# Epsilon of the first block's layer norms on VectorE, and token tile 0's normed rows ahead of token tile 1's first residual

## What is computed

```python
def layer_norm(x, g, b):
    mu = jnp.mean(xf, -1, keepdims=True)
    var = jnp.mean(jnp.square(xf - mu), -1, keepdims=True)
    return ((xf - mu) * lax.rsqrt(var + LN_EPS)).astype(x.dtype) * g + b
...
for l in range(DEPTH):                       # first block
    u = x * (1.0 + sc1) + sh1
    y = mixer(u, ...)                        # holds a layer norm of its own, of the convolution's rows
    x = layer_norm(DN_ALPHA * x + (1.0 + gt1) * y, ln_mix_g[l], ln_mix_b[l])
    u = x * (1.0 + sc2) + sh2
    h = jnp.square(jax.nn.relu(u @ w_up[l])) @ w_down[l]
    x = layer_norm(DN_ALPHA * x + (1.0 + gt2) * h, ln_ffn_g[l], ln_ffn_b[l])
```

## Time and profile before

| what | value |
|---|---|
| median of 3 runs | 1811.62 us (1811.55 to 1812.15) |
| span of the profiled execution | 1813.6 us |
| TensorE busy | 1755.5 us, 97% |
| VectorE busy | 1275.5 us, 70% |
| ScalarE busy | 891.5 us, 49% |
| GpSimd busy | 57.3 us, 3% |
| mean DMA rate over the span | 191 GB/s |
| mean granted TensorE clock | 0.997 of full |

### The profile page before, as it was taken

How to read it: one execution, slowest core, us unless ns; L and a number is a source line. 1 busy time by engine, 2 the same in 40 slices (tenths; PEclk the granted TensorE clock), 3 DMA queues, 4 the chain that set the end, 5 groups by cost and what they waited for, 6 DMA issues and landing times.

```text
span 1813.6 us, 26735 instructions
## 1 busy us (share of the span) xinstructions
PE 1755.5 (97%) x9254; PEld 1450.9 (80%) x9254; DVE 1275.5 (70%) x1973; ACT 891.5 (49%) x1530; POOL 57.3 (3%) x111
## 2 busy tenths in 40 slices
PE   8999999998999999998999999999999999999998
PEld 3776778996766779987998977788889989778886
DVE  5788887667788885568557987655555588865555
ACT  1456434443455444444556664544455667544443
POOL 0000010000000000002000000000000000000000
PEclk9999999999999999999999999999999999999999
DMA  8866568774866566663665444555646645345553
GB/s 300 267 213 218 162 216 301 253 230 133 264 220 209 185 210 209 209 190 110 210 215 156 131 142 141 174 185 184 190 153 200 215 131 160 117 155 182 184 186 126
DMA packets 216040, 346.29 MB, mean 191 GB/s; under 512 B 19611, under 2 KB 113353, under 8 KB 215673
## 3 DMA queue, kind: packets, MB, share of 16 engines
q1 hardware_dynamic: 213448, 338.89, 58.3%
q0 software_dynamic: 1632, 5.39, 1.0%
q10 hardware_dynamic: 850, 0.54, 0.1%
HBM read 343.69 MB, written 1.07 MB: 190 GB/s over the span
## 4 chain that ended last, share of the span: by engine, by line
issue 79%; PE 12%; DVE 4%; DVEq 1%; POOLq 1%; POOL 1%; ACT 0%; DMA 0%; SPq 0%; ACTq 0%
PE acc L150 2%; PE acc L148 2%; PE acc L149 2%; PE prod L223 1%; PE prod L225 1%; PE prod L224 1%; DVE w_lo L134 1%; DVEq L937 1%; PE prod L148 1%; DVE proj L938 1%; PE prod L150 1%; PE prod L149 1%; PE turn L262 0%; DVE x_res L938 0%; DVE x_res L936 0%
## 5 line engine op out<-in xcount | busy, mean ns | idle before, releaser
L134 DVE TENSOR_TENSOR w_lo<-w_raw,w_hi 128x1024 fp32r<-128x1024 f32 (+2 forms) x584 | 643.7, 1122 | 308.6 <-ACT w_hi L128 302.9
L128 ACT CAST w_hi<-w_raw 128x1024 fp32r<-128x1024 f32 (+2 forms) x584 | 557.9, 968 | 406.6 <-PE acc L150 186.3
L148 PE MATMUL prod<-w_hi,hT_hi 128*128 128x512 f32 (+2 forms) x880 | 319.8, 363 | 4.7 <-ACT proj_b L1949 3.6
L150 PE MATMUL prod<-w_hi,hT_lo 128*128 128x512 f32 (+2 forms) x880 | 313.0, 356 | 0.0
L149 PE MATMUL prod<-w_lo,hT_hi 128*128 128x512 f32 (+2 forms) x880 | 312.3, 355 | 0.0
L148 PEld LDWEIGHTS prod<-w_hi,hT_hi 128*128 128x128 f32 x880 | 166.3, 189 | 25.0 <-DVE gates L2202 5.9
L150 PEld LDWEIGHTS prod<-w_hi,hT_lo 128*128 128x128 f32 x880 | 166.3, 189 | 15.4
L149 PEld LDWEIGHTS prod<-w_lo,hT_hi 128*128 128x128 f32 x880 | 166.8, 189 | 14.6
L223 PE MATMUL prod<-uT_hi,w_hi 128*128 128x256 f32 x448 | 127.1, 284 | 1.6 <-DVE w_lo L134 1.1
L148 PE MATMUL prod<-w_hi,uT_hi 128*128 128x512 f32 x304 | 124.6, 410 | 2.7 <-DVE uT_lo L301 1.3
L224 PE MATMUL prod<-uT_lo,w_hi 128*128 128x256 f32 x448 | 126.4, 282 | 0.0
(11 more groups left out here) (349 smaller groups left out, 2836.6 us busy)
## 6 DMA issues: line engine op xcount, KB each, us to landing
w_raw<-in_w_in_dram SPq DMA_DIRECT2D x72, 512.0 KB, 3.8
ada_raw<-in_w_ada_dram SPq DMA_DIRECT2D x68, 512.0 KB, 6.7
w_raw<-in_w_in_dram SPq DMA_DIRECT2D x192, 172.0 KB, 2.4
w_raw<-in_w_up_dram SPq DMA_DIRECT2D x64, 512.0 KB, 4.4
w_raw<-in_w_down_dram SPq DMA_DIRECT2D x64, 512.0 KB, 4.5
w_raw<-in_w_gate_dram SPq DMA_DIRECT2D x128, 192.0 KB, 2.6
w_raw<-in_w_ffn_gate_dram SPq DMA_DIRECT2D x88, 256.0 KB, 3.6
w_raw<-in_w_ffn_up_dram SPq DMA_DIRECT2D x88, 256.0 KB, 4.3
```

What stands on the lines that cost most here:

```text
L128: act.copy(self.hi[:, s, 0:cols], self.raw[:, s, 0:cols]).then_inc(self.hi_done, 1)
L134: dve.tensor_tensor(self.lo[:, s, 0:cols], self.raw[:, s, 0:cols], self.hi[:, s, 0:cols].bitcast(F32), ALU.subtract).then_inc(self.lo_done, 1)
L148: pe.matmul(out, a_hi, w_hi, start=first and c == 0, stop=False)
L150: mm = pe.matmul(out, a_lo, w_hi, start=False, stop=last and c == chunks - 1)
```

## The change

Three things. `norm_rstd` on GpSimd loses the addition of epsilon and the drain; the root is its only instruction and is what waits for the signal. `mean_var` on VectorE gets the addition behind a drain, and the signal now comes from the addition. And at the four boundaries both normed halves of tile 0 stand ahead of the first residual half of tile 1. (Lines behind L694 move up by two on GpSimd, ScalarE and much of VectorE, and are equal again from L933 on.)

```diff
             def norm_rstd(n, ready, done, tok):

                 pool.wait_ge(ready, n)
-                pool.tensor_tensor(var_eps[:, tok:tok + 1], mv[:, tok, 1:2], eps, ALU.add)
-                pool.drain()
                 pool.tensor_tensor(rstd[:, tok:tok + 1], var_eps[:, tok:tok + 1], half_neg, ALU.pow).then_inc(done, 1)
...
             def mean_var(tok, parts, done):

                 dve.drain()
-                dve.bn_aggr(mv[:, tok, :], stats[:, tok, 0:parts, :].rearrange("p a s -> p (a s)")).then_inc(done, 1)
+                dve.bn_aggr(mv[:, tok, :], stats[:, tok, 0:parts, :].rearrange("p a s -> p (a s)"))
+                dve.drain()
+                dve.tensor_tensor(var_eps[:, tok:tok + 1], mv[:, tok, 1:2], eps, ALU.add).then_inc(done, 1)
...
                 mix_residual(0, 0)
                 mix_residual(0, 1)
                 split(layer(l, at + 8, G1), 1)
-                mix_residual(1, 0)
                 next_u2(0, 0)
                 next_u2(0, 1)
+                mix_residual(1, 0)
                 take_u2_lo(0)
                 mix_residual(1, 1)
                 split(layer(l, at + 9, G1), 2)
```

More of the change, by code:

```diff
@@ L1037, in vector @@
                     split(layer(l, 0, G1), 1)
-                    last_residual(1, 0)
                     next_u(0, 0)
                     next_u(0, 1)
+                    last_residual(1, 0)
                     take_u_lo(0)
```

## The result

| | kernel before | kernel after |
|---|---|---|
| median of 8 runs | 1811.69 us (1809.87 to 1815.61) | 1819.84 us (1815.68 to 1822.32) |
| ratio, 95% interval | 1 | 1.0037 (1.0028 to 1.0046) |
| span of the profiled execution | 1813.6 us | 1820.5 us |
| mean granted TensorE clock there | 0.997 | 0.995 |

The change makes the kernel slower by 0.37%, which is 6.7 us (5.1 to 8.3), against a forecast of 4.2. The sign and the mechanism were right. The two medians themselves are 8.2 us apart, at the upper end of that interval. The median of the kernel after lies 1.0 us above the upper end of the range; 1.0037 times the 1811.62 of the prediction is 1818.3, just inside it. That is not the place of the forecast's own case (1815.0 to 1816.6) but of its first rival, in which TensorE's clock falls (1817 to 1819).

A forecast was written before the change was run, and what follows sets the result against it. VectorE's queue was taken to bound the four boundaries, where norms stand between big products. Epsilon 2.2, root wait 2.1, sooner transposes 0 and convolution norms -0.1 sum to +4.2 us on 1811.62: 1815.8 us, range 1813.4 to 1818.8.

The forecast's parts named there:

- the forecast's own case: Whole kernel: VectorE's longer queue at the four boundaries gives 1815.0 to 1816.6 us; chance 0.52.
- first rival: TensorE's clock falls at its longer wait for the second `w_lo`, 1 us each fall, 1817 to 1819; chance 0.19.
- The reading of the bound: At the boundaries, time added to VectorE's queue between tile 0's aggregate and the second `w_lo` adds to the program.
- The wait for the root: At each boundary VectorE waits for GpSimd's root ahead of tile 0's normed rows: 0.53 us each, 2.1 in four.
- The holding by `w_lo`: A GpSimd operation begun inside a `w_lo` is held until that ends; a root then needs 0.40 us more.
- The rival of a root that isn't held: At the boundaries the root runs under `w_lo`, so 2.1 us go away: +2.1, 1813.7 us; chance 0.13.
- The epsilon term: Additions on VectorE at four boundaries, two tiles each: two at 0.20 and six at 0.30 us, 2.2 in all.
- Sooner transposes: Tile 0's transposes can start earlier at the boundaries, but TensorE then waits longer for the second `w_lo`: gain 0.
- The convolution norms: GpSimd's chain gets shorter there, but VectorE gains two additions of 0.30 and 0.26 us: minus 0.1 us together.
- a clock under 1 near 244 or 838 us: Sign of being wrong: granted TensorE clock under 1 near 244, 445, 644 or 838 us.
- dense neighbours of a lone pause: Argument against a clock fall: TensorE's wait at the second `w_lo` has dense products as neighbours.

The follow-up runs named there:

- the late wait: Kernel after, but VectorE waits for GpSimd's root only ahead of L938, not ahead of L936: median 1816.33 us, ratio 1.0023.
- epsilon alone: Kernel before with only the epsilon addition moved from GpSimd to VectorE, order of instructions unchanged: median 1816.06 us, ratio 1.0021.
- the reordering alone: Kernel before with only tile 0's normed halves put ahead of tile 1's first residual half, epsilon still on GpSimd: median 1818.95 us, ratio 1.0039.

## Why the prediction was right, and where it was short

**The reading of the bound held.** Where the clock held, what was put into VectorE's queue between the aggregate of tile 0 and the normed rows of tile 1 came out at the end of the boundary: 0.40 for two additions of 0.13 and 0.23, 1.03 for a wait of 0.96 and the 0.08 of lost overlap, 0.54 less when the wait went. Drawing the second `w_lo` forward only moved TensorE's wait, and the 0.26 us that it added to the queue stood at the third transposes. One correction: the prediction named the second `w_lo` as the place where the queue ends; it reaches further, to tile 1's normed rows, which changed no number.

**The wait for the root** was forecast at 0.53 a boundary and 2.1 in all. The row shows 0.46 of idle time and the 0.08 of overlap, 0.54. The holding by `w_lo`, on which it rests, was shown by taking `w_lo` away: 1.47 fell to 0.56. The rival of a root that isn't held has fallen. For tile 1 the prediction allowed for a root that is held by both `w_lo`, and even that would have cost nothing; the root is held by the first alone. It begins at 243.28 inside the first and, after 1.46 us, ends at 244.74, while the second still runs (243.12 + 2.35 = 245.47).

**The epsilon term was over-sized.** Forecast 0.30 for each of six additions and 0.20 for two, 2.2 us; the rows show 0.23 and 0.13, 1.6 us. The wrong step is the time from the start of the addition to the start of what follows: I took 0.14 from a row whose successor was a copy, and `w_lo` follows after 0.07 to 0.08.

**Sooner transposes** were priced at 0, and gave 0: the late wait at equal epsilon is as long as epsilon alone, 14.86, at the one boundary where both had a full clock.

**The convolution norms** gave 0.2 and 0.1 us, 0.3 together instead of 0.1, within the bounds given.

**A term was missing.** The two pauses, 0.42 and 0.36 us, lie on the path. With 1.6 for epsilon and 2.2 for the waits they make 4.6 of the 4.75 us by which the four boundaries grew at full clock. The forecast of 4.2 was thus near that sum in part by luck, because an over-sized term stood in for an unseen one. The page before does list pauses of this kind under "issue", but nothing in it told where they would fall in the changed kernel.

**The clock was under-weighted.** As the first rival it had a chance of 0.19 and a price of 1 us for each fall, and a clock under 1 near 244 or 838 us was named as a sign of being wrong; both came. It fell in two boundaries of the profiled kernel after, in three of the reordering alone and of the late wait, and in all four of others. The price was 0.72 us at one place and 0 at another, and 1.29 where `w_lo` had been drawn forward. What failed here is the chance: the prediction held dense neighbours of a lone pause for a protection, from the boundaries before at a wait of 1.35, and a wait of some 2 us no longer has it. The length of one wait doesn't decide it either: within the kernel after, waits of 2.48 and 2.15 passed at full clock, and the first boundary fell at 2.15. That the measured 1818.3 lies in this rival's case is luck too, since its two falls cost only 0.7 us together.

**What stays open.** 4.75 us at full clock, 0.7 for the clock and 0.3 back from the convolution make 5.2 us, inside the interval of the ratio (5.1 to 8.3) but at its lower end. Whether the remaining 1.5 us are falls of the clock in runs that were not profiled, pauses in other places or chance, these runs do not tell; the start alone differs by 4 us between profiles.

## What to carry to other kernels

Where one engine's queue is the path, a small instruction moved onto it is paid in full (here 0.23 us for one element a partition), while the engine that was relieved had its time hidden. An instruction that covers another engine's latency is not free to move: before drawing a consumer forward, ask what will stand between its producer and it. And if a wait is left, put it ahead of the first instruction that reads the result, not ahead of the group.

## What the runs showed of the hardware

- A GpSimd root of 128 numbers that begins inside a VectorE instruction with two SBUF inputs ends 0.40 to 0.43 us behind that instruction, however long it has waited: it takes 1.47 and 1.12 us behind wide and narrow `w_lo`, 0.91 beside a normed half, and 0.56 with VectorE idle. The next VectorE instruction does not hold it. An addition held by `w_lo` (1.21 us) ended 0.05 behind it (234.03 against 233.98).
- VectorE pauses for 0.36 to 0.54 us at fixed places of its instruction stream, in the same way in every profile of the same stream; between 100 and 900 us these places are multiples of 128 records apart in all 14 traces. An edit of a few instructions ahead can so cost or win 0.4 us at a place that it doesn't touch.
- Drains are not free: 60 in a row held VectorE for 3.0 us longer (the next memset started at 6.56 instead of 3.60), 49 ns each.
- A fall of the granted clock to 1.2 GHz for 3.4 us cost nothing where TensorE would soon have waited anyway, and 0.72 and 1.29 us elsewhere. It came after single waits of 2.15 us and also after two of 1.09 and 1.04.
